# Expert-gate quarter of the conditioning layer: multiplied during row dispatch instead of among the projections

## What is computed

```python
mod = (silu(c) @ w_ada + b_ada)[:, None, :]            # c: 9 conditioning vectors, w_ada: 1024 x 6144
sh1, sc1, g1, sh2, sc2, g2 = split(mod, 6, axis=-1)
h = rms_norm(x, norm1_w) * (1 + sc1) + sh1
z, xbc, dt, q, k, v, r, glr, ga, gb = split(h @ w_in, ...)
...                                                    # SSD branch, GLA branch, gated sum -> mixed
x = x + g1 * mixed
h2 = rms_norm(x, norm2_w) * (1 + sc2) + sh2
comb = route(h2)                                       # top 2 of 16 experts per token
y_moe = moe_ffn(h2, comb, w_exp_gate, w_exp_up, w_exp_down)
x = x + g2 * y_moe
```

## Time and profile before

| what | value |
|---|---|
| median of 3 executions | 1056.56 us (1056.18 to 1058.3) |
| the profiled execution, its own time | 1058.15 us |
| its span in the trace | 1055.8 us |
| TensorE (PE) busy | 1005.6 us, 95% of the span |
| VectorE (DVE), ScalarE (ACT), GpSimd (POOL) busy | 386.2, 233.0, 137.2 us |
| mean granted TensorE clock | 0.971 |
| DMA | 237.62 MB, mean 225 GB/s |

### The profile page before, as it was taken

The page is one execution under the profiler, slowest core; times in us unless marked ns, Lnnn a source line. Parts: engine busy times, 40 slices in busy tenths (PEclk is TensorE's granted clock), DMA queues, the critical chain, the costliest instruction groups (busy, mean ns, idle before and its releaser), DMA issues.

```text
span 1055.8 us, 20264 instructions
## 1 busy us (share of the span) xinstructions
PE 1005.6 (95%) x8523; PEld 754.8 (71%) x8523; DVE 386.2 (37%) x850; ACT 233.0 (22%) x466; POOL 137.2 (13%) x227
## 2 busy tenths in 40 slices
PE   5999999999989899999999999997799999999987
PEld 2667676676766566666676677666699999999951
DVE  3121235666435976656640701226111010110115
ACT  2130222332342232242251300003211010110012
POOL 0000233342000343323300000002000000000020
PEclk9999999999899899999999999998899999999995
DMA  9843346457353455656542633424749999999971
GB/s 379 316 191 119 124 156 235 135 199 244 125 187 139 178 191 196 228 178 216 186 142 94 252 125 128 147 102 142 271 141 389 398 419 405 397 403 388 414 274 52
DMA packets 47219, 237.62 MB, mean 225 GB/s; under 512 B 6800, under 2 KB 11344, under 8 KB 23856
## 3 DMA queue, kind: packets, MB, share of 16 engines
q1 hardware_dynamic: 45120, 230.85, 58.7%
q0 software_dynamic: 1472, 5.24, 1.6%
q10 hardware_dynamic: 560, 0.60, 0.2%
HBM read 212.31 MB, written 24.36 MB: 224 GB/s over the span
## 4 chain that ended last, share of the span: by engine, by line
PE 87%; DVE 3%; ACT 3%; DMA 3%; issue 2%; POOL 1%; ACTq 0%; DVEq 0%; SPq 0%; POOLq 0%
PE pjB L827 14%; PE pjA L827 14%; PE states L1370 10%; PE pjA L1218 7%; PE pjB L1218 7%; PE states L1373 5%; PE pjB L1370 3%; PE pjA L1370 2%; PE pjA L1373 1%; PE pjB L1373 1%; PE states L836 1%; PE bank L1182 1%; PE states L1197 1%; PE bank L951 1%; PE states L951 1%
## 5 line engine op out<-in xcount | busy, mean ns | idle before, releaser
L827 PE MATMUL pjB<-hF,ring 128*128 128x320 f32 x608 | 175.1, 442 | 0.0
L827 PE MATMUL pjA<-hF,ring 128*128 128x320 f32 x608 | 171.9, 436 | 0.5 <-ACT regA L1616 0.5
L1373 PE MATMUL states<-ring,oF 128*32 128x384 f32 x1392 | 155.5, 493 | 0.0
L1370 PE MATMUL states<-ring,oF 128*32 128x128 f32 x1392 | 155.5, 274 | 0.0
L1370 PEld LDWEIGHTS states<-ring,oF 128*32 128x32 f32 x1392 | 152.6, 111 | 0.7 <-issue 0.3
L827 PEld LDWEIGHTS pjB<-hF,ring 128*128 128x128 f32 x608 | 115.4, 193 | 50.1 <-issue 7.1
L827 PEld LDWEIGHTS pjA<-hF,ring 128*128 128x128 f32 x608 | 113.2, 190 | 50.6 <-issue 7.0
L2604 DVE TENSOR_TENSOR oF<-oF,states 128x384 f32<-128x384 f32 x15 | 8.3, 555 | 153.9 <-PE states L1373 153.9
L2336 DVE TENSOR_TENSOR G<-G 128x320 f32<-128x320 f32 x32 | 47.0, 1507 | 0.0
L1957 POOL TENSOR_TENSOR G<-regA,G 128x128 f32<-128x128 f32 (+1 forms) x32 | 19.0, 592 | 195.7 <-ACT G L1672 195.7
L1373 PE MATMUL pjB<-ring,hF 128*32 128x384 f32 x360 | 42.2, 493 | 0.0
(11 more groups left out here) (508 smaller groups left out, 1441.4 us busy)
## 6 DMA issues: line engine op xcount, KB each, us to landing
ring<-in_w SPq DMA_DIRECT2D x171, 1024.0 KB, 8.3
G<-in_ss SPq DMA_DIRECT2D x16, 512.0 KB, 4.0
out_ss_new<-G SPq DMA_DIRECT2D x16, 512.0 KB, 2.7
G<-csd SPq DMA_DIRECT2D x16, 320.0 KB, 3.5
G<-in_sg SPq DMA_DIRECT2D x4, 1024.0 KB, 6.5
out_sg_new<-G SPq DMA_DIRECT2D x16, 256.0 KB, 2.8
yd<-hF SPq DMA_DIRECT2D x14, 288.0 KB, 6.5
rF<-in_w SPq DMA_DIRECT2D x2, 1024.0 KB, 9.7
```

The source lines that it names most:

```text
L827: mm = pe.matmul(pj[g % 2][:, 0:T], w[:, k, half * P:half * P + P], hF[:, k, :], start=(k == 0), stop=(k == KT - 1))
L1370: pe.matmul(bank[CAP:P, c * P:(c + 1) * P], rows(c, True), w[:, WIDE:512], start=first and c == 0, stop=last, tile_position=(0, CAP), skip ...
L1373: mm = pe.matmul(bank[QUAD * c:QUAD * c + QUAD, 0:WIDE], rows(c, False), w[:, 0:WIDE], start=first, stop=last, tile_position=(0, QUAD * c) ...
```

## The change

The chunk order and the loop get a constant `LATE = 12`. Only the first 12 of the 16 later conditioning chunks stay in the loop; the last 4 (g2) stand in the chunk order after the output projection and before the experts. TensorE multiplies them after the ranks (L1327), two into each of the banks 2 and 3, the second pair after the first of DVE's six pieces. ACT copies each bank out in one instruction, four turns go side by side into bank 0, and DVE adds the bias in one instruction and makes `gsx`, both after `meta`. Waits for the number of finished conditioning parts fall from 17 to 13, and the wait for `s_gsx` moves to the transposes that need it.

```diff
     for i, c in enumerate(p2):
-        out += [c, ("ada", 8 + i)]
+        out += [c, ("ada", 8 + i)] if i < LATE else [c]
...
     out += [("out", c) for c in range(4)]
+    out += [("ada", 8 + i) for i in range(LATE, len(p2))]
...
-C_P3 = C_P2 + 32
+C_P3 = C_P2 + 16 + LATE
...
-C_MOE = C_OUT + 4
+C_ADA = C_OUT + 4
+C_MOE = C_ADA + 16 - LATE
...
-                return C_P2 + 2 * ((g - 16) // 2), g % 2
+                i = (g - 16) // 2
+                return C_P2 + i + min(i, LATE), g % 2
...
-                if s % 2:
+                if s % 2 and s < 2 * LATE:
                     pe.wait_ge(s_mod, 1 + s // 2)
                     ada(C_P2 + s, b[5])
-                elif s:
+                elif s and s % 2 == 0 and s <= 2 * LATE:
                     ada_turn(7 + s // 2, b[5][:, 256:256 + 2 * NSEQ])
...
-            ada_turn(23, b[5][:, 256:256 + 2 * NSEQ])
...
+            for i, bank in enumerate((b[2], b[3])):
+                if i:
+                    pe.wait_ge(s_htc, 1)
+                for j in range(2):
+                    ada(C_ADA + 2 * i + j, bank[:, 256 * j:256 * j + 256])
+            pe.wait_ge(s_htc, 2)
+            for j in range(4):
+                ada_turn(8 + LATE + j, b[0][:, 2 * NSEQ * j:2 * NSEQ * j + 2 * NSEQ])
 
             pe.wait_ge(s_htc, 6)
-            pe.wait_ge(s_gsx, 1)
             for n in range(12):
+                if n == 8:
+                    pe.wait_ge(s_gsx, 1)
...
+            for i, bank in enumerate((b[2], b[3])):
+                act.wait_ge(s_used, C_ADA + 2 * i + 2)
+                act.wait_ge(s_adt, 8 + LATE + 2 * i)
+                act.activation(adaS.rearrange("p a c -> p (a c)"), bank[:, :], ACT.Copy).then_inc(s_adc, 2)
...
             scales(32, V_N2)
-            dve.tensor_copy(gsx.rearrange("p k (s t) -> p k s t", t=ST),
-                            mod[:, 40:48, 1:].unsqueeze(3).to_broadcast([P, KT, NS, ST])).then_inc(s_gsx, 1)
...
             assert ds_.n == DISPATCH_META, ds_.n
+            dve.wait_ge(s_adt, 24)
+            dve.tensor_tensor(mod[:, 40:48, :], b[0][:, 0:8 * NSEQ].rearrange("p (a b) -> p a b", b=NSEQ),
+                              vec[:, 40:48].unsqueeze(2).to_broadcast([P, 8, NSEQ]), ALU.add).then_inc(s_mod, 1)
+            dve.wait_ge(s_mod, 2 + LATE)
+            dve.tensor_copy(gsx.rearrange("p k (s t) -> p k s t", t=ST),
+                            mod[:, 40:48, 1:].unsqueeze(3).to_broadcast([P, KT, NS, ST])).then_inc(s_gsx, 1)
```

More of the change, by code:

```diff
@@ L88 @@
     0, 2048, 4096, 4608, 5120, 5152, 5664, 6176, 7200, 8224, 8240, 9264)
+LATE = 12
 def weight_order():
@@ L682, in _ @@
             for s in range(N2 + LEAD):
-                if s < N2:
-                    load(C_P2 + s)
-                elif C_P2 + s < C_P3 + LEAD:
+                if C_P2 + s < C_P3 + LEAD:
                     load(C_P2 + s)
@@ L1193, in _ @@
                     pe.wait_ge(s_cbc, 3)
-                    pe.wait_ge(s_mod, 17)
+                    pe.wait_ge(s_mod, 1 + LATE)
                 for c in range(4):
@@ L1795, in _ @@
                                bias=vec[:, V_MRG + t:V_MRG + 1 + t]).then_inc(s_sil, 1)
-            act.wait_ge(s_mod, 17)
+            act.wait_ge(s_mod, 1 + LATE)
             act.activation(shX.rearrange("p k (s t) -> p k s t", t=ST),
@@ L2301, in _ @@
                                                         ALU.mult, ALU.mult))
-                if s and s % 2 == 0:
+                if s and s % 2 == 0 and s <= 2 * LATE:
                     c = 7 + s // 2
@@ L2420, in _ @@
             dve.wait_ge(s_x, 16 * 3)
-            dve.wait_ge(s_mod, 17)
+            dve.wait_ge(s_mod, 1 + LATE)
             scales(32, V_N2)
-            dve.tensor_copy(gsx.rearrange("p k (s t) -> p k s t", t=ST),
-                            mod[:, 40:48, 1:].unsqueeze(3).to_broadcast([P, KT, NS, ST])).then_inc(s_gsx, 1)
             dve.memset(os_, 0.0)
```

## The result

| | before | changed |
|---|---|---|
| median, us | 1056.37 (1055.03 to 1058.3, 4 executions) | 1062.48 (1061.48 to 1065.38, 4) |
| profiled execution, us | 1058.15 | 1065.38 |
| its span, us | 1055.8 | 1063.4 |
| its mean granted clock | 0.971 | 0.962 |

The ratio is 1.0071, 95% interval 1.0046 to 1.0096: slower, beyond what a measurement can mistake for no change. (Ratios and intervals are those on record with each run; they are not the quotients of the medians beside them, which here would be 1.0058.) The medians lie 6.1 us apart, where +4.9 was forecast. The changed kernel's profiled execution is its slowest; the other three had a clock of 0.970 or 0.971.

A forecast was written before the change was run, and what follows sets the result against it. DVE was taken to bound the loop's end, and DVE, POOL, scatter and readback the dispatch. -1.4 (loop) + 6.0 (transfers) + 0.3 (clock) = +4.9 us, forecast 1061.5 us, 0.46% slower; range 1055.5 to 1064.6.

The forecast's parts named there:

- What bounds the kernel: Projection loop's end: DVE, then POOL, from 337 us; dispatch: DVE, POOL, scatter and readback; TensorE at neither.
- Sum: 0.26 + 1.00 + 0.16 = 1.4 us earlier: End of the projection loop: steps 25, 27 and DVE's two additions bring the row at 359.31 forward by 1.4 us.
- I take 0: Half clock after the loop, from 359 us: no net effect, between 0.6 us worse and 1.6 us better.
- the loop gives nothing: Rival, projection loop: new idle time brings the half clock early and eats the 1.4 us; 1062.9 us; chance 0.05.
- Cost of both: 0: Dispatch: the added work of TensorE and DVE hides in waits, TensorE's transposes starting at about 732.5; cost 0.
- If that cover failed, it would be 0.3 us: Dispatch: TensorE's cost if its added work were not hidden by its waits, 0.3 us.
- +6.0: Dispatch: four expert loads collide with scatter and readback; first token block later by +6.0 us, between +4.4 and +7.1.
- the packet rival: Dispatch: queues take turns by packets, scatter gets 37% and comes last; +7.1 instead of +6.0, 1062.6 us; chance 0.20.
- +0.3: Clock from 744 us: after a longer idle time, half clock lasts 1.7 us more or no longer; +0.3 us taken.
- the fastest rival: Dispatch, 741 to 744 us: tokens not held up, price 0; with shorter half clock at 360 us 1053.6 us; chance 0.10.
- the rival of no change: Dispatch: tokens not held up, without the help of the clock; 1055.2 us, no change; chance 0.06.
- The sign against me at the expert stage: Expert stage, first to last down product: a change of over 1 us would show a cost not named.

The follow-up runs named there:

- e1: Changed kernel without its four late chunks, neither loaded nor multiplied (g2 is the bias alone): 1054.84 us, ratio 0.9994.
- e3: Changed kernel with the store of the convolution states (`conv_new`) moved ahead of the last loads: 1063.1 us, ratio 1.0081.
- e4: Changed kernel with the loads of expert chunks 2 to 5 issued after the readback of the tokens: 1054.44 us, ratio 0.9987.
- e8: e4 again, with more rounds, on another chip: 1058.75 us, ratio 1.0028.
- e10: The changed kernel again, unaltered, with more rounds: 1061.3 us, ratio 1.0076.
- e2: Kernel before, with only its last four loads ahead of the experts held until the ranks are counted: 1061.57 us, ratio 1.0069.
- e7: e2 with the wait moved two chunks ahead, so that seven loads are held back: 1068.79 us, ratio 1.0129.
- e6: Changed kernel with the four last chunks multiplied right behind step 31 of the projection loop, expert loads early again: 1053.2 us, ratio 0.9974.
- e9: e6 again: 1051.62 us, ratio 0.9977.

## Why the prediction was right, and where not

The sign was right, the time near (+4.9 us forecast, +6.1 measured), and the two places were the right ones. The two main terms were off by a similar amount and to the same side (the loop gave 1.1 us less, the transfers cost 1.2 more), so the time was not right by their cancelling.

- **What bounds the kernel.** Right. TensorE reached the first `x_turn` 6.78 us earlier (6.7 by the sum), but the row behind POOL's product moved by 1.0 (changed) and 1.3 us (e1) only; DVE's norm and the load of the states behind it were the limit, and the rest became the wait of 6.34 us. The words "TensorE did 6.7 us less" misread their own sum: the four chunks and turns are 5.4 us of work, and its 3.70 holds 1.66 and 0.50 us in which TensorE was idle.
- **"Sum: 0.26 + 1.00 + 0.16 = 1.4 us earlier".** Right at its row. "I take 0" for the clock behind it was wrong in sign: the half clock took back 1.6 us in the changed kernel's profile (0.99 gained, 0.60 lost at the next head pair) and 0.9 in e1's, both more than the bound of 0.6 us. Over all profiles, the first piece starts at 727.45 us in the six with the changed loop (changed, e1, e3, e4, e8, e10) and at 727.74 in the three with the old one (before, e2, e7), 0.3 us for the loop within a spread of 3.2. The rival "the loop gives nothing" (0.05) was nearer than my forecast here, though neither the 0.36 us of e1 nor these 0.3 can be told from its zero. The Trainium skill's advice against idle stretches ("TensorE: Matmul & The Clock Gate", part 1) deserved more than the bounds that I gave it: the clock in that window was 0.77 before and 0.55, 0.68 and 0.60 in the changed kernel, e10 and e1.
- **"Cost of both: 0"** for the work at the dispatch. Right in the time, since the tokens came later still; wrong in its working. The first transposes started at 734.55 us, not 732.5; they did not run "at full clock" (0.53 granted from 734.5 to 741 us); and the last ended at 745.15, 3.6 us later than before (2.9 counted from the first piece). Against that stood not the "2.85 us to spare" but about 1.1, by the 1.72 us that e4 and e8 show behind the last transpose. The later readback covered it. "If that cover failed, it would be 0.3 us" was too small: e8 shows a distance 3.55 us longer with the cover gone, e4 1.20. In e8 ACT's late copies (last section) are a part of it.
- **Transfers, "+6.0".** The mechanism was right: full engines from 729 to 747, the readback behind. The size was off by about 1.2 us, and it was the choice in the middle that failed: the scatter came last, as the packet rival (0.20) had it, and its +7.1 us is what e10 (+7.14) and the first profile (+7.25) show. The 34% of the engines measured answer to the 37% worked out there, which took 6.2 KB for a packet of the loads from a mean with 390 packets of under 512 B in it; beside the scatter they have 7.3 KB. The row to lean on was the two packet sizes in rows 10; halves of the engines' time was a guess between the ends.
- **The clock at 744, "+0.3".** Neither shown nor excluded. Over the 7 us from the first token transpose the granted clock was 0.76 before, 0.62 in the changed kernel's first profile and 0.76 in e10's. From that transpose to the first L1373 (L1385) with `oF` it took 23.55 us before, 24.44 and 23.60 in those two: +0.9 once and nothing once.
- **The range.** It was to leave out "no more than the fastest rival", but ends at 1055.5, which also leaves out the rival of no change at 1055.2 (0.06).

- **The signs named ahead.** The wait of some 6 us (6.34), the full engines from 729 to 747 and the late token transpose (752.31, at the end of "749 to 752") were there. The pieces "1 to 2 us earlier" were 0.6 later in the first profile and 2.6 earlier in e10's. The sign against me at the expert stage did not come: its products (L1373, in the changed kernel L1385) stretch over 269.5 us before and 269.4 in e10.

With the measured sizes the sum is -0.3 + 7.2 = +6.9 us; the medians say 6.1.

## What to carry to other kernels

Before work is moved to where an engine is idle, ask for each of its transfers when it was issued until now and what will be in flight there afterwards; the loads that inherit its buffers move with it. A scatter or gather on the critical path with small packets beside a bulk load gets a share by packets, not by bytes, so it may land last although it moves less (here 2.62 MB beside four loads of 1.05 MB); keep bulk loads ahead of it or behind its reader. Before an engine's wait is counted as room, ask what else that engine has to do in it: of 2.85 us some 1.1 were free. And an idle stretch of the array is better filled than made longer: the same four chunks cost 6 us at the dispatch, and in the hole that the loop had they cost nothing and may have gained some 3.

## What the runs showed that I had not expected

- **Equal turns to the packet.** 464 against 466 packets over 12 us (e7), 150 against 148 over 4 us (changed kernel).
- **Executions of one kernel differ by a clock that falls or does not** in the same stretch: some 4 of the 8 us between e6's and e9's profiles, with idle times that differ by 0.2 us.
- **ACT stands still where nothing visible holds it.** In the profiles of e10, e3, e4 and e8, all with the four chunks' work at the dispatch, one of its copies starts 1.5 to 2.3 us later than it could. Timeline of ACT, e10:

```profile
732.20 0.60 ACT L1838 ACTIVATE G<-bank 128x512 f32<-128x512 f32 x1 [2.21 <-PE states L1354]
735.13 0.60 ACT L1838 ACTIVATE G<-states 128x512 f32<-128x512 f32 x1 [2.34 <-remote]
```

The bank `states` was full at 732.03. That wait is what makes TensorE late behind it (its 2.30 us above). The kernel before has the like in a copy that TensorE does not wait for. Timeline of ACT, before:

```profile
736.87 0.59 ACT L1821 ACTIVATE G<-states 64x512 f32<-64x512 f32 x1
738.88 0.60 ACT L1821 ACTIVATE G<-pjA 128x512 f32<-128x512 f32 x1 [1.43 <-PE pjB L1345]
```

`pjA` was full at 737.62 there and ACT free at 737.46, so this copy is 1.26 us late. So the standstill is not the change's own; with the four chunks at the dispatch it falls on an earlier copy. The DMA view has one packet of instructions (queue q8) from 732 to 736 us both in e10 and before; whether it has to do with it is not known, and the cause stays open.
